# Norms that turn x by a diagonal, a first product pass by pass, packed score levels, and ScalarE's tables loaded by hand

## What is computed

```python
def rmsnorm(x, g):
    y = xf * lax.rsqrt(jnp.mean(xf * xf, axis=-1, keepdims=True) + EPS)
    return (y * g).astype(x.dtype)

# HGRN2, one chunk: scores between tokens t >= s, with decays b (a running sum of log f)
rel = jnp.exp(jnp.where(causal, bi[:, :, :, None, :] - bi[:, :, None, :, :], -jnp.inf))
scores = jnp.einsum("bhtd,bhsd,bhtsd->bhts", qi, ki, rel)

for l in range(DEPTH):
    h = rmsnorm(x, norm_mix[l])
    p = h @ w_in[l]                       # then groups A (HGRN2), B, C, D
    x = x + concat(y_a, y_b, y_c, y_d) @ w_out[l]
    x = x + memory_cross_attention(rmsnorm(x, norm_xattn[l]), mem_n, ...)
    h = rmsnorm(x, norm_ffn[l])
    x = x + (swiglu(h, ...) if l % 2 == 0 else moe_swiglu(h, ...))
return rmsnorm(x, norm_final)
```

## Time and profile before

| | |
|---|---|
| median of 3 runs | 2117.27 us (2116.48 to 2118.86) |
| the profiled execution's own time | 2117.68 us, of which span 2115.8 us |
| TensorE busy | 1922.4 us (91%) |
| VectorE busy | 1480.4 us (70%) |
| ScalarE busy | 1143.3 us (54%) |
| mean granted TensorE clock | 0.941 of full |

### The profile page before, as it was taken

One profiled execution on the slowest core, in us unless ns is written; L12 is line 12 of the kernel. 1 busy time (PEld: TensorE's weight loads), 2 busy tenths in 40 slices (PEclk: granted clock), 3 DMA queues, 4 the chain that ended last, 5 costly groups with the idle time before them and its releaser, 6 DMA issues.

```text
span 2115.8 us, 28844 instructions
## 1 busy us (share of the span) xinstructions
PE 1922.4 (91%) x12072; PEld 1637.5 (77%) x12073; DVE 1480.4 (70%) x1565; ACT 1143.3 (54%) x1078; POOL 0.2 (0%) x4
## 2 busy tenths in 40 slices
PE   6987789889998987789869999999999999999996
PEld 6975677779997966578748888888888888888884
DVE  6776544354447686535369888889888898988885
ACT  5543304343434643214357777767777776777773
POOL 0000000000000000000000000000000000000000
PEclk9997789989998998789979999999999999999998
DMA  7531003235554530003249999999999999999992
GB/s 227 173 127 40 22 22 113 86 114 189 193 193 123 179 102 22 20 22 120 80 157 384 346 358 338 378 334 368 355 337 364 333 387 328 369 357 340 358 374 83
DMA packets 238774, 466.06 MB, mean 220 GB/s; under 512 B 11056, under 2 KB 87088, under 8 KB 238640
## 3 DMA queue, kind: packets, MB, share of 16 engines
q1 hardware_dynamic: 238640, 464.16, 61.8%
HBM read 463.09 MB, written 1.05 MB: 219 GB/s over the span
## 4 chain that ended last, share of the span: by engine, by line
PE 83%; DVE 12%; ACT 3%; issue 2%; DVEq 0%; DMA 0%; ACTq 0%
PE ps L1887 29%; PE ps L1477 16%; PE ps L1897 14%; PE ps L1462 11%; PE ps L1495 7%; DVE MT L812 4%; PE ps L1943 1%; PE ps L1957 1%; PE ps L1918 1%; PE ps L1465 1%; DVE MT L815 1%; DVE hT_lo L818 1%; DVE TMP L812 1%; DVE MT L1032 1%; DVE MT L818 1%
## 5 line engine op out<-in xcount | busy, mean ns | idle before, releaser
L1253 DVE TENSOR_TENSOR wlo<-raw,whi 128x2048 fp32r<-128x2048 f32 x140 | 320.2, 2290 | 70.7 <-ACT whi L694 70.6
L694 ACT ACTIVATE whi<-raw 128x2048 fp32r<-128x2048 f32 x140 | 268.8, 1921 | 130.8 <-PE ps L1897 77.6
L825 DVE TENSOR_TENSOR wlo<-raw,whi 128x2048 fp32r<-128x2048 f32 x85 | 194.5, 2289 | 131.8 <-ACT whi L429 131.7
L1253 DVE TENSOR_TENSOR wlo<-PT,whi 128x2048 fp32r<-128x2048 f32 x84 | 192.1, 2291 | 33.6 <-ACT whi L694 33.6
L429 ACT ACTIVATE whi<-raw 128x2048 fp32r<-128x2048 f32 x85 | 161.9, 1905 | 55.9 <-PE ps L1495 46.7
L1887 PE MATMUL ps<-whi,hE_hi 128*128 128x512 f32 x672 | 185.4, 398 | 2.4 <-DVE hE_lo L1319 2.4
L694 ACT ACTIVATE whi<-PT 128x2048 fp32r<-128x2048 f32 x84 | 161.4, 1922 | 34.7 <-PE ps L1887 34.0
L1887 PE MATMUL ps<-wlo,hE_hi 128*128 128x512 f32 x672 | 180.1, 390 | 0.0
L1887 PE MATMUL ps<-whi,hE_lo 128*128 128x512 f32 x672 | 179.8, 389 | 0.0
L1477 PE MATMUL ps<-hT_hi,whi 128*128 128x256 f32 x928 | 136.3, 291 | 23.2 <-DVE hT_lo L818 23.2
L1887 PEld LDWEIGHTS ps<-wlo,hE_hi 128*128 128x128 f32 x672 | 126.2, 188 | 27.1
(11 more groups left out here) (259 smaller groups left out, 3313.9 us busy)
## 6 DMA issues: line engine op xcount, KB each, us to landing
raw<-in_moe_w_up SPq DMA_DIRECT2D x111, 1024.0 KB, 6.8
PT<-in_moe_w_down SPq DMA_DIRECT2D x56, 1024.0 KB, 6.5
PT<-in_moe_w_gate SPq DMA_DIRECT2D x55, 1024.0 KB, 6.7
TMP<-in_moe_w_gate SPq DMA_DIRECT2D x55, 1024.0 KB, 6.7
raw<-in_moe_w_down SPq DMA_DIRECT2D x55, 1024.0 KB, 6.4
raw<-in_w_in SPq DMA_DIRECT2D x28, 1024.0 KB, 5.5
raw<-in_ffn_w_gate SPq DMA_DIRECT2D x11, 1024.0 KB, 5.3
raw<-in_ffn_w_up SPq DMA_DIRECT2D x11, 1024.0 KB, 5.4
```

The lines of the kernel that those rows point to most:

```text
L694: nc.scalar.activation(ex_hi[m % XSPL], ex_raw[m % XRAW], ACT.Copy).then_inc(S("w_hi"), 1)
L825: V.tensor_tensor(wlo[i % SPL][:, :], raw[d % RAW][:, :], whi[i % SPL][:, :].bitcast(F32), ALU.subtract).then_inc(S("w_lo"), 1)
L1253: V.tensor_tensor(ex_lo[m % XSPL], ex_raw[m % XRAW], ex_hi[m % XSPL].bitcast(F32), ALU.subtract).then_inc(S("w_lo"), 1)
```

## The change

It has four parts.

1. **Norms.** DVE no longer scales x. It makes `diag(t)`, the unit matrix times the reciprocal roots (128 x 128), and PE computes x times that diagonal in 16 plain fp32 matmuls, which turns and scales at once. The turned blocks lie two to a bank in banks 4 to 7 (`turned_x`). Of the eight `hT_hi` blocks ACT writes 0, 1, 4, 5 and DVE 2, 3, 6, 7, and then DVE all eight `hT_lo`. DVE's Newton step is one instruction shorter and partly ahead of the root. For the experts, which need `xs` in token order, DVE makes it behind the norm. The last norm applies its gain in the same instruction and is stored tile by tile.
2. **First product.** Of each norm's product the first chunk goes pass by pass over both halves (`first_product`), and each block is waited for when its turn comes. The router's product does the same. In the cross attention the last 3 of 8 steps of a `kv` product are put between the turn and the first product.
3. **Packed levels.** At levels 0 to 5 only 64 x 64 blocks on the diagonal are computed (`scores_b`); queries and keys share one tile, so that two half-size products replace two whole ones; `take` is one instruction over two banks. The last level has only the cross block (`scores_cross`, two plain copies). `outputs_b` reads this layout, and the products of the last steps of `hgrn` stand in another order.
4. **Tables.** `table(...)` loads a set by hand at a chosen place, ahead of the waits of what needs it; there are 40 loads in all.

```diff
-                    tt(col(t), col(t), col(6 + t), ALU.mult)
-                    ts(dst[:, t, :], src[:, t, :], col(t), ALU.mult).then_inc(S("n_xs"), 1)
+                    if dst is None:
+                        ts(diag(t), ident, col(t), ALU.mult, col(6 + t), ALU.mult).then_inc(S("n_xs"), 1)
...
             def norm(i, gain, dst):
                 ahead(2)
+                for c in HI_DVE:
+                    dve.wait_ge(S("n_tr"), trunk(i) * KT + c // 2 * 2 + 2)
+                    ts(dst[0][:, c, :], turned_x(c), gain(c), ALU.mult).then_inc(S("n_lo"), 1)
                 for c in range(KT):
-                    dve.wait_ge(S("n_hi"), (i - (i > MEM_NORM)) * KT + c + 1)
-                    stt(dst[1][:, c, :], ps[:, c, 0:SEQ], gain(c), dst[0][:, c, :].bitcast(F32), ALU.mult, ALU.subtract).then_inc(S("n_lo"), 1)
+                    if c in HI_ACT:
+                        dve.wait_ge(S("n_hi"), hi_ready(i, c // 2 * 2 + 1)[1])
+                    stt(dst[1][:, c, :], turned_x(c), gain(c), dst[0][:, c, :].bitcast(F32), ALU.mult, ALU.subtract).then_inc(S("n_lo"), 1)
...
-                        tr(ps[:, c, P * t:P * t + P], xs[:, t, P * c:P * c + P]).then_inc(S("n_tr"), 1 if t else 0)
-                pe.wait_ge(S("n_lo"), (i + 1 - (i > MEM_NORM)) * KT)
+                        mm(turned_x(c)[:, P * t:P * t + P], x[:, t, P * c:P * c + P], diag(t)).then_inc(S("n_tr"), 1 if t else 0)
+
+            def first_product(n, bank, i):
+                wp = [chunk_view(v[n % SPL][:, :], "cm") for v in (whi, wlo)]
+                pe.wait_ge(S("w_hi"), n + 1)
+                for p_, (a_, b_) in enumerate(PASSES):
+                    if p_ == 1:
+                        pe.wait_ge(S("w_lo"), n + 1)
+                    for k in range(KT):
+                        if p_ == 0:
+                            sem, count = hi_ready(i, k)
+                            pe.wait_ge(S(sem), count)
+                        if p_ == 2:
+                            pe.wait_ge(S("n_lo"), lo_ready(i, k))
+                        for m in range(2):
+                            ins = pe.matmul(ps[:, bank, SEQ * m:SEQ * m + SEQ], wp[a_][:, k, P * m:P * m + P], hT[b_][:, k, :],
+                                            start=p_ == 0 and k == 0 and m == 0, stop=p_ == 2 and k == KT - 1 and m == 1)
+                ins.then_inc(S("chunk_done"), 1)
...
-                    tt(H(4 + v % 2), pt(A_Q), tmp(6 + v % 2), ALU.mult)
-                    tt(H(v % 2), tmp(0), tmp(6 + v % 2), ALU.mult).then_inc(S("hg_qk"), 1)
+                    halves = lambda ap: ap.rearrange("p (n u h) -> p n u h", u=2, h=1 << v)
+                    for u, of in ((0, tmp(0)), (1, pt(A_Q))):
+                        tt(halves(H(v % 2))[:, :, u], halves(of)[:, :, u], halves(tmp(6 + v % 2))[:, :, u], ALU.mult).then_inc(S("hg_qk"), u)
...
-                rglru(l, LEVELS)
                 dve.wait_ge(S("state"), 3 * l + 1)
                 tt(tmp(5)[:, 256:512].rearrange("p (c n) -> p c n", c=2), ps[:, 6, 0:256].rearrange("p (c n) -> p c n", c=2),
                    rep(bdones, 2), ALU.mult).then_inc(S("state_bd"), 1)
+                rglru(l, LEVELS)
...
             def experts():
-                stats(6, x, xs)
+                stats(6, x)
                 norm(6, lambda c: pc("norm_ffn", 1, c), hT)
+                for t in range(TT):
+                    ts(xs[:, t, :], x[:, t, :], col(t), ALU.mult, col(6 + t), ALU.mult).then_inc(S("n_xs"), 1)
```

More of the change, by code:

```diff
@@ L417, in _, with table @@
             split = [0]
+            def table(name):
+                nc.scalar.preload_act_table_set(name)
             def a(o, i, f, **kw):
@@ L528, in logs @@
                 o, o2 = PCOL["gdn_A_log", l][0], PCOL["lru_lambda", l][0]
+                table("exp_and_others")
                 act.wait_ge(S("gd_x"), l + 1)
@@ L579, in hgrn @@
                     a(G_N[j], ps[:, j, :], ACT.Ln, bias=epsc(0))
+                act.wait_ge(S("hg_trk"), l + 1)
+                a(tmp(5)[:, 0:256], ps[:, 5, 0:256], ACT.Copy).then_inc(S("hg_kd"), 1)
+                a(H(11), H(11), ACT.Exp, scale=0.5).then_inc(S("lru_root"), 1)
                 for j in range(2):
                     a(G_N[j], G_N[j], ACT.Exp, scale=-0.5).then_inc(S("gd_rn"), 1)
+                table("natural_log")
                 head_rms(l, 0, 7)
@@ L590, in head_rms @@
                 a(tmp(7), tmp(7), ACT.Exp, scale=-0.5).then_inc(S("o_rn"), 1)
+                if which:
+                    table("natural_log")
             def rwkv_ahead(l):
@@ L667, in swiglu @@
                 stats(3, x, 2)
+                table("silu_and_others")
                 norm(3, lambda c: pc("norm_ffn", 0, c), hT)
@@ L684, in experts @@
                 stats(6, x, 5)
+                table("sigmoid_and_others")
                 norm(6, lambda c: pc("norm_ffn", 1, c), hT)
@@ L800, in _ @@
             experts()
+            table("sqrt_and_others")
             act.wait_ge(S("x_done"), 11)
@@ L1533, in small_product @@
                     for kk in range(KT):
+                        if i_norm is not None and i == 0:
+                            sem, count = hi_ready(i_norm, kk)
+                            pe.wait_ge(S(sem), count)
+                        if i_norm is not None and i == 2:
+                            pe.wait_ge(S("n_lo"), lo_ready(i_norm, kk))
                         ins = pe.matmul(ps[0:8, bank, 0:SEQ], small[a_][:, kk, :], hT[b_][:, kk, :],
@@ L1631, in hgrn @@
                 pe.wait_ge(S("state_bd"), 3 * l + 1)
-                outputs(7, [(tmp(1), mt(1))], tmp(5)[:, 256:512], H(4)).then_inc(S("o_full"), 1)
+                outputs_b(7, tmp(1), mt(1), tmp(5)[:, 256:512], H(4)).then_inc(S("o_full"), 1)
                 head_ss(l, 0)
```

172 lines of the change are left out of this document (119 added, 53 removed).

## The result

The changed kernel took **2068.4 us** (median of 4, 2067.5 to 2069.3), the kernel before on the same chip 2118.0 (4 runs): ratio **0.9766** (95% interval 0.9750 to 0.9781). The forecast was 2073, with 2062 to 2092. The profiled execution took 2069.3, its span is 2067.4 against 2115.8: 48.4 us, which the two traces let one lay out by stretches. Such a ledger is made by taking the start of the same instruction in both traces at every seam and writing down how the difference grows ("squares" is the start of ScalarE's first square of a norm, "second chunk" the start of the second chunk's product).

A forecast was written before the change was run, and what follows sets the result against it. The prediction put 83% of the chain that ended last on TensorE, with time to be had only at the seams. Its terms, 10.6 + 10.4 + 3.8 + 13.5 + 0.8 + 5.0 = 44.1, took 2117.5 to 2073 us, range 2062 to 2092.

The forecast's parts named there:

- HGRN2: Both layers' levels and the way to the outputs: 13.5 us gained (7 to 17), 7.6 and 5.9 by layer.
- the first norm: Norm at the start: product starts at 17.7 instead of 22.66; 3.8 us gained (2 to 6).
- the experts' norm: Norm ahead of the experts: earlier turn, later logits copy, no load ahead of the sigmoid; 0.8 us gained (-2 to 3).
- the last norm: Kernel's end: no table load, one fused VectorE instruction, stores of half the size; 5.0 us gained (4 to 5.5).
- groups B to D: Stretch behind HGRN2 up to cross attention: loads there lie behind other waits or only move; nothing gained.
- Norms at a pause: Feed-forward of layer 0 and mix of layer 1: earlier turn, clock rising midway; 5.3 us each, 10.6 together.
- the new turn counts as work: Turns at the pauses: matmuls bring full clock, transposes do not; 6.0 us gained with this rule, -0.5 without.
- Cross attention's norms: Two norms: kv matmuls fill the hole, so TensorE's clock stays; 5.2 us each, 10.4 together.
- 1 us off: First norm: small product waits for VectorE's third wlo and the memory norm, pushed back by late lo blocks; 1 us lost.
- the rival of the full clock: HGRN2's norm sums, outputs and kv behind: full clock where it was half, 4.5 us less a layer, 2064; chance 0.15.
- The load ahead of the sigmoid, 1.28, is gone: Behind the experts' norm: the table load of 1.28 us leaves the path, within that norm's 0.8 us.
- The packed copy: HGRN2's `take` with repeated mask runs off its pace: at 5.7 us a piece all 44 gone, at 8, 2145; chance 0.03.

The follow-up runs named there:

- the transposes experiment: The changed kernel with TensorE turning x by 16 transposes instead of 16 fp32 matmuls by the diagonal, reciprocal roots missing: 2062.4 us (ratio 0.9738).
- the last kernel: The changed kernel with three reorderings (experts' norm, first norm, HGRN2's end), scaled x turned by transposes, and the square ahead of the table load: 2055.3 us (0.9702).
- The doubled scores: The changed kernel with the packed scores of levels 0 to 5 issued twice on TensorE: 2074.9 us (0.9799).
- the experiment: The changed kernel without table loads, the compiler placing each ahead of the first function that needs it: 2077.4 us (0.9814).
- one call in the wrong place: The changed kernel with the end of the RG-LRU (`rglru`) ahead of the masked state again: 2080.0 us (0.9822).

## Why the prediction was right, step by step

The total (44.1 forecast, 48.4 in the profiled execution) is right within 10%, but it is a sum of steps that are off in both directions: HGRN2 gave 7.7 more than forecast, and the first norm, one of the pauses, the experts' norm, the last norm and groups B to D together some 5 less. That these offset each other is luck.

- **Norms at a pause.** Forecast 5.3 each, measured 5.4 and 4.5. The mechanism is the one named: earlier turn, no hole, clock back in the middle. The reason given beside it, that the new turn counts as work where transposes do not, is what the transposes experiment refutes for this kernel, so the 5.3 was right for a reason that was partly wrong. The Trainium skill ("TensorE: Matmul & The Clock Gate", Part 4: PE-mode transpose), by which transposes do not bring the full clock, is not borne out where they stand without a hole ahead of matmuls: there the full clock came as it did with the matmuls. In the transposes experiment 1.8 us of product lay ahead of the rise, in the last kernel's pause only 0.3 behind 3.3 us of transposes. A rise with no matmul at all behind the transposes no run shows.
- **Cross attention's norms.** 5.2 forecast, 5.5 and 5.4 measured, with the turn at full clock.
- **The first norm.** 3.8 forecast, 2.35 in this trace, 2.7 to 3.4 by the start of the second chunk in the eight others that start alike. The product itself did better than forecast: it ended at 25.25, 5.8 earlier than before, where 4.7 was put. What was too small is the "1 us off" for what stands behind it: the small product waits 1.83 for VectorE's split of the small weights, and in this trace the granted clock is 0.50 from 27.9 to 31.2 and that product runs at half pace. For the first 27 us the granted clock reads 1.00 in both traces, though 8 matmuls took 1.91 at 24.53 in the kernel before, where 1.12 is the full pace; the forecast's "half clock for the first 6 us, as before" is read off the durations and not off the granted clock.
- **HGRN2** is the term that was mis-sized: 13.5 forecast, 21.2 measured (11.1 and 10.1). The step is "64 x 64 blocks in four quadrants, 16 for 8, I price at the same 1.16". They take 0.69, so TensorE's floor is 4.28 and not 4.75. Over the levels that is 8.2 in layer 0 (162.77 - 128.00 against 152.13 - 125.60) where 5.1 was forecast; layer 1 missed by about as much, so the levels make up some 6 of HGRN2's 7.7. The doubled scores put the floor back to 4.74, to within 0.01 of the forecast's. The Trainium skill ("TensorEngine Tiling (Array Packing)", Key Properties) states that different tiles, of which the array holds four of 64 x 64, can load and multiply in parallel; by it twice the matmuls, each with half the columns and in four tiles instead of two, would cost half of 1.16, an estimate of 0.58. The 0.69 of the trace is much nearer to that than to the 1.16 of the forecast.
- **Behind the levels** two errors partly cancel. From level 6 to the outputs 5.7 was put; it takes 8.1, because the copy of the keys waits for a load of 1.28 and three Ln, and the squares and exponentials ahead of them start only behind the put of kv 3. On the other side the stretch from the outputs to group B gave 1.3 in layer 0 and 1.2 in layer 1, where the forecast took 0.5 off for it. That is part of the rival of the full clock: half clock still came in this stretch (161.1 to 167.9 in layer 0), but lasted 6.8 us instead of some 10.
- **Experts' norm.** 0.8 forecast, 0.0 measured. The copy of the logits came 0.6 later behind the squares than before (0.5 forecast). What failed is "The load ahead of the sigmoid, 1.28, is gone": before, it ran from 1081.15 to 1082.43 while VectorE worked on the operand until 1082.26, so its removal brought only 0.2. From the copy to the first expert product it is 17.8 instead of 18.4.
- **Last norm.** 5.0 forecast, 4.3 measured; the second tile's small steps start only behind the first tile's product of 1.28, so it is done 6.1 behind the squares where 5.2 was put.
- **Tables.** Priced at 1.28 each on the path, 9 in all by the experiment. The Trainium skill ("ScalarE: Activation LUTs", What ACT_TABLE_LOAD costs) has a drain of 1.38 on top; here the row of the load stands 0.02 behind what is ahead of it and 0.02 ahead of the root, and the 9 in all leave no room for it.
- **The packed copy**, the rival on the other side, takes 0.73 for 512 elements with its repeated mask: no penalty.
- **Experts.** Their 1004.8 from the first product to the last squares are unchanged, as was said.
- **Groups B to D**, put at nothing, took 1.8 in layer 0 and gave 0.5 in layer 1, where the change moves only table loads. In layer 0 half clock lasted 61.5 us of them instead of 54.6. In layer 1 it lasted longer too, 61.4 instead of 58.0, and TensorE idled 0.9 less; what gave the 0.5 is not shown.

## What to carry to other kernels

Where one engine writes an operand in parts and TensorE waits for the whole, let the product go pass by pass: here taking it away cost 35 of 49.6, since it closes a hole in which the clock falls as well. Then look at what now stands in the queue ahead of the critical instruction: a table load or a weight split that cost little under the old hole was worth 1 to 3.4 us each afterwards, and one call in the wrong place 12 over two layers. Price a change of shape on TensorE by how much of the array its blocks leave free, not by the count of instructions: 16 blocks of 64 x 64 took 0.69 where 8 of 64 x 128 took 1.16.

## What was not expected of the hardware

- Sixteen fp32 matmuls of 64 x 64 by 64 columns, in four quadrants (32 records), take 0.69, eight of 64 x 128 by 128 columns take 1.16, and 32 of the small ones take 1.16 too.
- In a turn at half clock, transposes of 128 x 128 took 3.65 for 16 and fp32 matmuls of the same size 5.90, partly at full clock already; at full clock matmuls took 3.81. The full clock returned 5.1 and 4.4 us behind their starts. In the last kernel's pause it returned 3.6 us behind the start of a turn by transposes.
- The same groups B to D of layer 0 ran in 156.6 to 158.5 us, with half clock for 54.6 to 61.5 us of them, in kernels that differ only ahead of them. So a change far ahead can move a stretch by up to 2 us either way.
